# A 13-step lockstep in place of 14 in the chunked RWKV-7 recurrence of a hybrid decoder layer

## The reference, cut to what matters

```python
S = S * w_t[:, :, None, :] + sa[..., None] * b_t[:, :, None, :] + v_t[..., None] * k_t[:, :, None, :]   # sa = S a_t
y = jnp.einsum("bhij,bhj->bhi", S, r_t)
...
xpad = jnp.concatenate([buf0, glu], axis=1)                    # convolution beside it, 31 taps, causal, per channel
y = lax.conv_general_dilated(xpad, conv_w, padding="VALID", feature_group_count=C_CONV) + conv_b
```

## Time and profile before

| | |
|---|---|
| median of 3 runs | 1090.45 us (1088.4 to 1091.57) |
| profiled execution, its own time | 1088.82 us |
| its span, first to last instruction | 1087.1 us |
| mean granted TensorE clock in the span | 0.998 |
| TensorE matmul busy | 1068.1 us, 98% |
| VectorE busy | 559.9 us, 51% |
| ScalarE busy | 447.5 us, 41% |
| GpSimd busy | 348.4 us, 32% |
| chain that ended last | PE 81%, DVE 8%, ACT 4% |

### The profile page before, as it was taken

One profiled execution on the slowest core, in us unless ns is written; L12 is line 12 of the kernel. 1 busy time (PEld: TensorE's weight loads), 2 busy tenths in 40 slices (PEclk: granted clock), 3 DMA queues, 4 the chain that ended last, 5 costly groups with the idle time before them and its releaser, 6 DMA issues.

```text
span 1087.1 us, 26532 instructions
## 1 busy us (share of the span) xinstructions
PE 1068.1 (98%) x11415; PEld 1007.2 (93%) x11415; DVE 559.9 (51%) x990; ACT 447.5 (41%) x780; POOL 348.4 (32%) x174
## 2 busy tenths in 40 slices
PE   8999999999999999999999999999999999999998
PEld 7998899998998997999999679899999999999998
DVE  5488788777785757874642943633232232200004
ACT  6454534434443677335553525723222222222232
POOL 3431331322311400645332003313344344344450
PEclk9999999999999999999999999999999999999999
DMA  7321121221213443565247783312323332332322
GB/s 221 90 77 34 58 61 42 60 78 41 68 41 114 124 137 96 196 199 150 59 156 236 245 315 94 97 54 79 92 83 94 96 89 84 92 88 87 92 68 80
DMA packets 163757, 115.96 MB, mean 107 GB/s; under 512 B 5304, under 2 KB 153034, under 8 KB 163401
## 3 DMA queue, kind: packets, MB, share of 16 engines
q1 hardware_dynamic: 159979, 104.87, 31.5%
q10 hardware_dynamic: 3686, 9.75, 2.5%
HBM read 108.91 MB, written 6.17 MB: 106 GB/s over the span
## 4 chain that ended last, share of the span: by engine, by line
PE 81%; DVE 8%; ACT 4%; issue 3%; DMA 2%; POOL 1%; DVEq 0%; ACTq 0%; POOLq 0%
PE ps L514 53%; PE ps L969 11%; PE ps L496 10%; PE ps L1614 3%; DVE conv_y L2477 2%; POOL w_lo L837 1%; DMA cache<-in_cache_mem_v_dram 1%; DVE cache L2913 1%; ACT w_hi L550 1%; DVE ps L2826 1%; DMA x_tok<-in_x_prompt_dram 1%; PE ps L558 0%; DVE m_lo L594 0%; DVE y_buf L2897 0%; PE ps L916 0%
## 5 line engine op out<-in xcount | busy, mean ns | idle before, releaser
L837 POOL TENSOR_TENSOR w_lo<-w_raw,w_hi 128x1024 fp32r<-128x1024 f32 (+2 forms) x122 | 287.7, 2359 | 562.8 <-ACT w_hi L550 562.8
L514 PE MATMUL ps<-h_hi,w_hi 128*128 128x260 f32 x1324 | 277.7, 291 | 1.3 <-POOL w_lo L837 1.0
L514 PE MATMUL ps<-h_hi,w_lo 128*128 128x260 f32 x1324 | 266.3, 283 | 0.0
L514 PE MATMUL ps<-h_lo,w_hi 128*128 128x260 f32 x1324 | 266.1, 282 | 0.0
L514 PEld LDWEIGHTS ps<-h_hi,w_hi 128*128 128x128 f32 x1324 | 204.2, 188 | 11.3 <-issue 5.5
L514 PEld LDWEIGHTS ps<-h_hi,w_lo 128*128 128x128 f32 x1324 | 204.0, 188 | 0.0
L514 PEld LDWEIGHTS ps<-h_lo,w_hi 128*128 128x128 f32 x1324 | 203.6, 188 | 0.0
L550 ACT ACTIVATE w_hi<-w_raw 128x1024 fp32r<-128x1024 f32 (+2 forms) x132 | 130.6, 991 | 165.0 <-PE ps L514 158.5
L2477 DVE SCALAR_TENSOR_TENSOR conv_y<-glu,prm,conv_y 128x512 f32<-128x512 f32 x120 | 103.9, 866 | 2.5
L2811 DVE TENSOR_TENSOR sq_acc<-sq_acc,sq_tmp 128x264 f32<-128x264 f32 (+2 forms) x35 | 28.0, 800 | 116.1 <-ACT sq_tmp L2343 76.0
L3018 DVE TENSOR_TENSOR f_tmp<-ps,silu 128x520 f32<-128x520 f32 x19 | 13.3, 699 | 137.7 <-PE ps L514 137.7
(11 more groups left out here) (497 smaller groups left out, 2090.0 us busy)
## 6 DMA issues: line engine op xcount, KB each, us to landing
w_raw<-in_w_gate_up_dram SPq DMA_DIRECT2D x44, 512.0 KB, 3.7
w_raw<-in_w_in_dram SPq DMA_DIRECT2D x38, 512.0 KB, 3.7
cache<-in_cache_mem_k_dram SPq DMA_DIRECT2D x16, 512.0 KB, 6.4
cache<-in_cache_mem_v_dram SPq DMA_DIRECT2D x16, 512.0 KB, 6.4
w_raw<-in_w_down_dram SPq DMA_DIRECT2D x16, 512.0 KB, 4.1
w_raw<-in_w_k_dram SPq DMA_DIRECT2D x8, 512.0 KB, 4.1
w_raw<-in_w_v_dram SPq DMA_DIRECT2D x8, 512.0 KB, 3.7
w_raw<-in_w_out_dram SPq DMA_DIRECT2D x8, 512.0 KB, 4.1
```

The lines of the kernel that those rows point to most:

```text
L514: mm = nc.tensor.matmul(ps[:, 2 * s + a, 0:width], w[:, k, :], x[:, x0 + k, a * width:(a + 1) * width], start=(first and k == 0 and n == 0 ...
L837: pool.tensor_tensor(lo[:, 0:kts], w_raw[:, b % RAW_SLOTS, 0:kts], hi[:, 0:kts].bitcast(F32), ALU.subtract).then_inc(w_lo_ready, 1)
```

## The change

`gram_b` and `gram_a` become one step, `gram_ab`. Per group TensorE issues the eight 64x128 products and then the eight 64x64 products, which go to the next 64 columns of the same PSUM regions. VectorE takes them out with three instructions: `mask_t` product into `AT`, `mask_s` product into `PW` and `RB`, and then, behind a wait for that, `XI = PW + identity`, whose end releases the step. So the lockstep has 13 names. The 24 dense slices are shared over 13 entries, 3 behind each of the two Gram steps and 2 behind `tok` and `akv`. The first pair does three taps instead of two ahead of the lockstep and one fewer behind `akv`; the tap that stood between `gram_k` and `gram_a` stands behind `gram_k`. The other pairs keep their taps in number: they had none between the Gram steps and have none now.

```diff
-STEP_ENGINES = [("gram_b", "v"), ("gram_k", "v"), ("gram_a", "v"), ("tok", "a"), ("akv", "a"),
+STEP_ENGINES = [("gram_ab", "v"), ("gram_k", "v"), ("tok", "a"), ("akv", "a"),
...
-LOCK_FILL = [n for fill in (2, 2, 2, 2, 2, 1, 2, 1, 2, 2, 1, 1, 2, 2) for n in (0, fill)]
+LOCK_FILL = [n for fill in (3, 3, 2, 2, 1, 2, 1, 2, 2, 1, 1, 2, 2) for n in (0, fill)]
...
-TAP_LEAD = (2, 4)
-TAP_FILL = ((0, 0, 0, 1, 0, 0) + (3, 3, 2, 2) + (1,) * 7 + (2, 0, 0, 1, 1) + (1, 1, 0, 4, 1, 0),
...
+TAP_LEAD = (3, 4)
+TAP_FILL = ((0, 0, 0, 1) + (3, 3, 2, 1) + (1,) * 7 + (2, 0, 0, 1, 1) + (1, 1, 0, 4, 1, 0),
...
-                if name in ("gram_b", "gram_k"):
+                if name in ("gram_ab", "gram_k"):
                     for c, n, i, odd, h in four:
-                        lhsT = bi[fm(h), c, 0, :] if name == "gram_b" else kt_fm[fm(h), c, :]
+                        lhsT = bi[fm(h), c, 0, :] if name == "gram_ab" else kt_fm[fm(h), c, :]
                         mm = small(region(rows(h, odd, False), i, h, 0, 2 * HS), lhsT, ar[fm(h), c, :, :])
-                elif name == "gram_a":
-                    for c, n, i, odd, h in four:
-                        mm = small(region(rows(h, odd, False), i, h, 0, HS), ar[fm(h), c, 0, :], bi[fm(h), c, 0, :])
+                    if name == "gram_ab":
+                        for c, n, i, odd, h in four:
+                            mm = small(region(rows(h, odd, False), i, h, 2 * HS, 3 * HS), ar[fm(h), c, 0, :], bi[fm(h), c, 0, :])
...
-                if name in ("gram_b", "gram_k"):
+                if name == "gram_ab":
+                    m = mask_t[:, 0, :].unsqueeze(1).unsqueeze(1).to_broadcast([P, 2, 2, HS])
+                    tt(pairs(big[:, cs, AT]), both(base, 2 * HS, 3 * HS), m, ALU.mult)
+                if name in ("gram_ab", "gram_k"):
                     m = mask_s[:, :, :].rearrange("p a n -> p (a n)").unsqueeze(1).unsqueeze(1).to_broadcast([P, 2, 2, 2 * HS])
-                    dst = big[:, cs, 2 * HS:4 * HS] if name == "gram_b" else g2[:, cs, :]
+                    dst = big[:, cs, 2 * HS:4 * HS] if name == "gram_ab" else g2[:, cs, :]
                     ins = tt(pairs(dst), both(base, 0, 2 * HS), m, ALU.mult)
-                elif name == "gram_a":
-                    dve.wait_ge(step_v, emptied("v", p, q + 1))
-                    tt(big[:, cs, XI], big[:, cs, PW], stack_id[:, :].unsqueeze(1).to_broadcast([P, 4, HS]), ALU.add)
-                    m = mask_t[:, 0, :].unsqueeze(1).unsqueeze(1).to_broadcast([P, 2, 2, HS])
-                    ins = tt(pairs(big[:, cs, AT]), both(base, 0, HS), m, ALU.mult)
+                    if name == "gram_ab":
+                        link_v(ins)
+                        ins = tt(big[:, cs, XI], big[:, cs, PW], stack_id[:, :].unsqueeze(1).to_broadcast([P, 4, HS]), ALU.add)
```

More of the change, by code:

```diff
@@ L102 @@
 assert sum(LOCK_FILL) == 3 * KT and sorted(LOCK_END.values()) == [0, 1, 2]
-TAP_LEAD = (2, 4)
-TAP_FILL = ((0, 0, 0, 1, 0, 0) + (3, 3, 2, 2) + (1,) * 7 + (2, 0, 0, 1, 1) + (1, 1, 0, 4, 1, 0),
-            (0,) * 6 + (3, 3, 2, 1) + (1,) * 7 + (2, 0, 0, 1, 1) + (1, 1, 0, 4, 1, 0))
+TAP_LEAD = (3, 4)
+TAP_FILL = ((0, 0, 0, 1) + (3, 3, 2, 1) + (1,) * 7 + (2, 0, 0, 1, 1) + (1, 1, 0, 4, 1, 0),
+            (0,) * 4 + (3, 3, 2, 1) + (1,) * 7 + (2, 0, 0, 1, 1) + (1, 1, 0, 4, 1, 0))
 assert all(lead + sum(fill) == TAPS and len(fill) == N_LOCKSTEP for lead, fill in zip(TAP_LEAD, TAP_FILL))
```

## The result

The changed kernel takes 1092.54 us (median of 19 runs), the kernel before 1090.29 in as many runs beside it. The ratio is 1.0025, 95% interval 1.0017 to 1.0032: slower by 2.7 us, between 1.9 and 3.5. The forecast was 1093.5 us and 0.28%, range 1088.5 to 1096. The profiled execution has a span of 1090.8 us at a granted clock of 0.998, as before.

What follows compares the result with a forecast made beforehand. TensorE's matmuls, busy 98% of the span, were taken to bound the kernel. 4 x 1.23 us lost ahead of `tok` less 1.8 given back made +3.1 us: 1091.9 for the profiled execution, 1093.5 as median, range 1088.5 to 1096.

Steps and rivals of the forecast that it cites:

- What bounds the kernel: TensorE, its matmuls busy for 98% of the span, sets the time; waits in its row come out nearly whole.
- TensorE's own work: From the lockstep's head to `tok`: 7.34 us instead of 7.57, saving 0.23 us a pair, 0.9 over four.
- The hold: Ahead of `gram_k`: GpSimd's subtraction holds VectorE's identity addition; TensorE waits 0.58 and 0.88 us, together 1.46 a pair.
- What is given back: At `dbl1`: TensorE's waits for VectorE go, 0.87 + 0.26 + 4 x 0.16 = 1.8 us.
- The tap at the front: Ahead of pair 1's first Gram product: a 0.75 to 0.8 us tap fits VectorE's 1.28 us idle, costing nothing.
- Not held: Rival: the identity addition is not held, so no wait ahead of `gram_k`; -2.6 us, 1087.8 us; chance 0.13.
- Nothing given back: Rival: holds stay; moved taps and GpSimd's second subtraction meet anew at `dbl0`; 4.9 us, 1095.4 us; chance 0.14.
- later stages took anything up: Rival: holds stay, but later stages absorb delay where TensorE waits for something else; some 1 us left, 1091.5; chance 0.10.
- The sum: Whole kernel: 4 x 1.23 - 1.8 = +3.1 us, 1091.9 us for the profiled execution, 1093.5 as a median.
- chance of 0.41 for more than 0.3%: Whole kernel above 1093.7 us: four tenths of the likeliest case (0.63) and all of the "Nothing given back" rival.

Runs made afterwards that it cites:

- fourth run: Changed kernel, with ScalarE rounding the last weights only after VectorE's `gram_ab`, so GpSimd's subtraction starts later; ratio to the kernel before 1.0003.
- second run: Changed kernel, with the third output multiplying the product in PSUM by the identity instead of adding two SBUF inputs; ratio to the kernel before 0.9976.
- first: Changed kernel, with the identity addition moved from `gram_ab` to behind `gram_k`, ahead of the `g2` product; 1086.29 us, ratio to the kernel before 0.9969.
- the tap alone: Kernel before, with only the tap change: three taps ahead of the first pair's lockstep, one fewer behind `akv`; ratio to the kernel before 1.0001.

## Why the prediction was right

- **What bounds the kernel.** Right: 98% as before, and TensorE's waits of 5.4 us, less what is won elsewhere in its row, come out in the time.
- **TensorE's own work.** Right in kind, too small: 0.23 us a pair forecast, 0.32 measured where nothing waits (7.57 to 7.25). The merged step takes 1.49 us where 1.65 were booked: a half that stands between other small matmuls is shorter (0.23 us for the first 64x64 half, 0.44 for the second 64x128 half) than the mean of a step of its own (0.31 and 0.52). The slices and the `gram_k` round took 0.06 more than booked.
- **The hold.** Right, and shown: the addition at 2.1 us after the head (2.09 in three pairs, 2.44 in the fourth), 2.40 us long (2.06), ended 0.28 after GpSimd; it goes with GpSimd (fourth run), with the SBUF input (second) and with the place (first). Its price was 1.65 us a pair against 1.46 forecast. Of the difference 0.1 is that TensorE was ready earlier, and 0.1 lies behind the second wait: from the start of `gram_k`'s second group to `tok` 2.95 us passed (153.95 to 156.90), 2.85 were booked. `tok` at 8.90 against 8.80.
- **What is given back.** Right: 1.1 us at `dbl1` itself and 4 x 0.19 behind it, 1.9 against 1.8.
- **The tap at the front.** Its cost of nothing is shown by the tap alone: the head stays at 7.57 us.
- **The rivals.** "Not held" describes the second run, which took what that rival would have: 2.6 us less, between 1.4 and 3.8. "Nothing given back" did not come; nor is there a sign that later stages took anything up: the span grew by 3.7 us, the locksteps by 2.6.
- **The sum.** +3.1 us forecast, +3.4 by one profile each (+2.6 with the third pair as it stands), +2.7 by the timed runs with an interval that holds all three. Whether it is above or below 0.3% the runs do not settle. The prediction's chance of 0.41 for more than 0.3% is a little over what its own terms give, 0.4 x 0.63 + 0.14 = 0.39.

## What to carry to other kernels

Before an output is put earlier on VectorE, look where its inputs lie and what GpSimd does at that time: here 0.42 us became 2.40 by moving one instruction with two SBUF inputs 3.75 us forward (from 5.84 to 2.09 us after the head), and one input from PSUM, or a place behind the next product, made it 0.42 again. When steps are merged, what releases the merged step should be only what the next step needs; `XI` was not needed until `dbl1`. A wait that vanishes is won only while one engine stays behind the other; ask of each variant anew which of the two comes last.

## What the runs showed of the hardware beyond what was expected

- In the merged step the switch from 64x128 to 64x64 products added nothing: from its first record to the next product the first 64x128 half takes 0.49 us in the traces of both kernels, with 64x64 products behind it or with 64x128. 16 records of 64x64 came to 0.23 us between other small matmuls, 0.28 directly behind dense slices and 0.34 with the change to the slices behind them.
- A VectorE addition with two SBUF inputs, issued 0.27 or 0.62 us into GpSimd's subtraction, took 2.40 or 2.06 us: it ended 0.28 to 0.29 us after GpSimd either way.
- When VectorE was first by 0.06 us, GpSimd's subtraction became 2.61 us long instead of 2.39, and a second addition, issued 1.33 us into it, ended 0.28 after that longer end (1.56 us).
- TensorE's wait for the memory values, between 632 and 653 us of the span, was 0.6 to 2.8 us in profiles of kernels that do not differ there, and 0.6 and 2.5 in two of the same kernel.
